# A decoder layer on one core: the feed-forward norm's root ahead of two projection copies, and three weight blocks' low parts subtracted on GpSimd

## The chip, the cores and the metric

The kernel runs on one core of a Trainium2 chip. The metric is the device time of one launch in microseconds, the median of several runs. The profile is one profiled execution; in its rows PE is TensorE (PEld its weight loads), DVE is VectorE, ACT is ScalarE, POOL is GpSimd and SP is SyncE, which only issues DMAs here.

## The reference

One decoder layer works on 512 prompt positions and 8 sample positions, 520 columns in all, with a width of 2048 and a feed-forward width of 5632. Cut to what matters here:

```python
def layer_out(h, o_sb, o_cm, p, g_out_sb, g_out_cm, w_out, g_ffn, w_gate, w_up, w_down,
              g_ple, w_ple_gate, w_ple_proj):
    o = jnp.concatenate([rmsnorm(o_sb, g_out_sb), rmsnorm(o_cm, g_out_cm)], axis=-1)
    h = h + o @ w_out
    f = rmsnorm(h, g_ffn)                # mean square over 2048 features, its root, then the gain
    h = h + (jax.nn.silu(f @ w_gate) * (f @ w_up)) @ w_down
    h = h + jax.nn.sigmoid(rmsnorm(h, g_ple) @ w_ple_gate) * (p @ w_ple_proj)
    return h
```

Before it, a mixer (attention and a gated MLP inside chunks) makes o_sb and o_cm. All is in fp32.

## The kernel before

**Layout.** Activations lie feature-major: 16 tiles of 128 features by 520 columns. Each fp32 number is split in a high part (fp32r, written by ScalarE) and a low part (the number less its high part, written by VectorE), for weights and activations alike; a product is then three matmuls: high by high, high by low, low by high. TensorE multiplies blocks of 128 by 128 by 260 columns.

**Order of the stages around the change.** After the output projection (TensorE L2113), `p @ w_ple_proj` is computed, 16 tiles of 12 matmuls (L2348, `plain_block`), while the residual's norm is finished. ScalarE copies each finished tile out of PSUM (`take_proj`, L1280) and GpSimd sends it to DRAM (L978). A tile n of TensorE waits for copy n-2. In the same time ScalarE squares the last residual tiles (`square_residual`, L1130) and multiplies them by the gain (`weigh_residual`, L1138); GpSimd has summed the first 15 squares in `h_sum`. TensorE sums over the partitions by matmuls with ones (L2459 for `h_sum`, L2460 for tile 15's squares), and ScalarE makes the root by Ln and Exp (L1420, L1421), which counts `root_done`.

**The first pair.** Gate and up tiles are computed in pairs, by a scheme of seven products (blocks 0 to 6 of a pair, `product`, L2364) in place of eight. Each product wants a weight block (128 by 1024) and an operand (half of the features by half of the columns), and both are sums or differences of halves. For the weights VectorE makes the sums (`add_weights`, L1825, into `w_sum` or the raw weights), ScalarE the high part (`high_pair`, L1293) and VectorE the low part (`low_pair`, through `low`, L1813). For the operands, once for the whole feed-forward part, VectorE scales f by the root (`scale_op`, L2004), combines quarters (`combine_op`, L2009), ScalarE makes the high part (`high_op`, L1285), VectorE the low part (`low_op`, L2016), all in two halves g = 0, 1. The order on VectorE and on ScalarE is written out by hand for the first pair. `pair_of_tiles` then runs for each pair; for the first one with `begun=True`, which leaves out what was written out by hand.

**Who waits for whom.** `lo_done` counts low parts of weights in order. TensorE waits for it before each product (`after_low`), VectorE before it writes over `w_sum` or a raw block, and SP before it loads the next weights into a raw slot. ScalarE writes block k's high part once product k-3 has ended, as three blocks fit into the buffer. TensorE's product 0, 1 and so on of a pair go into three accumulators, and product 2 waits until ScalarE has copied part 0 (`copy_part`, L1335). At the end of a gate tile ScalarE applies Silu (L1387 to L1390), with a load of its table, and then takes part 0 of the next pair.

Of the kernel before, what the change touches and what calls it, by code (L numbers as in the profile page):

```python
# [76 lines left out]
DOWN_COPIES = 5  # L77
PROJ_JOBS = 4
UNIT_JOBS = 7
DOWN_JOBS = 4 * UNIT_JOBS  # L80
CHUNK_COPIES = 4 * DOWN_COPIES

# [295 lines left out]
def build(nc, w_units, x_t, p_t, cache_k, cache_v, page_table, g_mix, g_out, g_ffn, g_ple, g_q, g_k,  # L378
# [6 lines left out]
    with ExitStack() as ctx:  # L385
# [156 lines left out]
        def raw(i):  # L542
            return raw_slot(LOADS[i].slot)
# [4 lines left out]
        def slot(w, job):  # L548

            first = JOB_POS[job] % SUBS * SUB  # L550
            return w[:, :, :].rearrange("p a n -> p (a n)")[:, first:first + JOB_SIZE[job] * SUB]
# [327 lines left out]
        def _(pool):  # L879
# [96 lines left out]
            for n in range(KT):  # L976
                pool.wait_ge(proj_taken, n + 1)
                pool.dma_start(proj_dram[:, n, :], proj_stage[:, n % STAGES, :]).then_inc(proj_out[n % STAGES], 16)  # L978
            def residual(u, row, half):

                first = 4 * u + 2 * row
                return h_dram[:, first:first + 2, half * HALF:(half + 1) * HALF]
# [37 lines left out]
        def _(act):  # L1020
# [106 lines left out]
            def square_residual(k):  # L1127

                act.wait_ge(h_final, k + 1)
                act.activation(f[:, k, :], h[:, k, :], ACT.Square).then_inc(sq_done, 1)  # L1130

            def weigh_residual(k):

                if k == KT - 1:
                    act.wait_ge(x_sum_ready, 4)
                else:
                    act.wait_ge(h_sum_done, k + 1)
                act.activation(f[:, k, :], h[:, k, :], ACT.Copy, scale=gain_ffn[:, k:k + 1]).then_inc(f_done, 1)  # L1138
# [136 lines left out]
            def take_proj(n):  # L1275

                act.wait_ge(ended, n + 1)
                if n >= STAGES:
                    act.wait_ge(proj_out[n % STAGES], 16 * (n // STAGES))
                act.activation(halves(proj_stage[:, n % STAGES, :]), tile_ps(n), ACT.Copy).then_inc(proj_taken, 1)  # L1280
# [130 lines left out]
            high_w(U_FFN + 1, 0)  # L1411
            weigh_residual(KT - 4)
            weigh_residual(KT - 3)
            take_proj(0)
            square_residual(KT - 1)
            weigh_residual(KT - 2)
            take_proj(1)
            take_proj(2)
            act.wait_ge(x_sum_ready, 4)
            chained(act.activation(halves(h_r[:, :]), pair, ACT.Ln, bias=eps[:, 0:1], scale=1.0 / D_MODEL))  # L1420
            act.activation(h_r[:, :], h_r[:, :], ACT.Exp, scale=-0.5).then_inc(root_done, 1)  # L1421
            take_proj(3)
            high(3, slot(w_hi, 3), raw_slot(3))
            take_proj(4)
# [75 lines left out]
        def _(dve):  # L1500
# [326 lines left out]
            def low_pair(item, k):  # L1827

                src = {0: raw(item.loads), 3: raw(item.loads + 3), 4: raw(item.loads + 1),
                       6: raw(item.loads + 2)}  # L1830
                low(item.jobs + k, src[k] if k in src else w_sum[:, :])
# [70 lines left out]
            def join(dst, x, w):  # L1902
                dve.tensor_tensor(dst, x, w, ALU.add).then_inc(joined, 1)

            def pair_of_tiles(item, after, acc, begun=False):
# [37 lines left out]
                dve.wait_ge(ended, item.end + 4)  # L1943
                dve.wait_ge(copied, 4 * item.n + 1)
                join(part[:, 0, :], part[:, 0, :], y_acc)
                begin(after, 1)
                dve.wait_ge(copied, 4 * item.n + 4)
                join(part[:, 2, :], part[:, 2, :], part[:, 3, :])
# [111 lines left out]
                combine_op(quad(1, 0, g), quad(0, 0, g), -1.0, quad(1, 0, g), 11 + g)  # L2060
            for g in range(2):
                low_op(4, g, quad(0, 1, g))
            low_pair(first, 4)
            for g in range(2):
                low_op(5, g, quad(1, 1, g))
            low_pair(first, 5)
            for g in range(2):
                low_op(6, g, quad(1, 0, g))
            low_pair(first, 6)

            for item, after in zip(ITEMS, ITEMS[1:]):
                if isinstance(item, Down):
# [33 lines left out]
        def _(pe):  # L2106
# [35 lines left out]
            def wait_free(free, reader):  # L2142
                if free[0]:
                    pe.wait_ge(*free[0])
                free[0] = reader
# [293 lines left out]
                    mm.then_inc(ended, 1)  # L2439


            pe.wait_ge(p_lo_done, 2)
            for n in range(KT):
                job = n // 4
                if n % 4 == 0:
                    after_low(job)
                if n < 2:
                    pe.wait_ge(out_read, T_FFN - 1 + n)
                else:
                    pe.wait_ge(proj_taken, n - 1)  # L2450
                for k in range(2):
                    plain_block(job, n % 4 * 2 + k, tile_ps(n), p_hi[:, k, :], p_lo[:, k, :], k == 0, k == 1)
                if n == 1:
                    pe.wait_ge(h_sum_done, KT - 1)
                    pe.wait_ge(sq_done, X_SQUARES + 3 * HEADS + KT)
                    wait_free(pair_free, (root_done, 4))
                    for a in range(2):
                        half = slice(a * HALF, (a + 1) * HALF)
                        pe.matmul(pair_ps[:, a, 0:HALF], ones[:, :], h_sum[:, half], start=True, stop=False)  # L2459
                        mm = pe.matmul(pair_ps[:, a, 0:HALF], ones[:, :], f[:, KT - 1, half], start=False, stop=True)  # L2460
                    mm.then_inc(x_sum_ready, 1)


            pe.wait_ge(root_done, 4)
# [131 lines left out]
```

## Time and profile before

| | us |
|---|---|
| median of 3 runs (2404.16 to 2405.17) | 2404.69 |
| the profiled execution's own time | 2404.58 |
| its span in the trace | 2402.8 |
| TensorE busy | 2369.7 |
| VectorE busy | 1777.4 |
| ScalarE busy | 1201.4 |
| GpSimd busy | 377.8 |

Times in the rows below are microseconds from the span's start. The own time is 1.78 us more than the span. The stretch of interest lasts from about 828 us, where the projection begins, to about 905 us, in the second pair.

### The profile page before, as it was taken

To read this page: it belongs to the slowest core of one execution; us is meant where nothing else is said; L and a number is where in the kernel's file an instruction comes from. 1 tells how busy PE (TensorE), PEld (TensorE's weight loads), DVE (VectorE), ACT (ScalarE), POOL (GpSimd) and SP (SyncE) were. 2 spreads that over 40 slices of the span, in tenths; PEclk is the share of its full clock that TensorE was granted. 3 is DMA by queue.
4 is the path that set the end of the run, shared out by engine and by line. 5 is a ranking of instruction groups with operands and counts; after the bars stand their busy time and mean duration, and the time that the engine had idled before them with its cause. 6 is when DMAs were issued, how large, how long until landed. Compare 5 with 4: busy or idle time off the path is not lost.

```text
span 2402.8 us, 46846 instructions
## 1 busy us (share of the span) xinstructions
PE 2369.7 (99%) x19392; PEld 2346.2 (98%) x19392; DVE 1777.4 (74%) x2209; ACT 1201.4 (50%) x1935; POOL 377.8 (16%) x364
## 2 busy tenths in 40 slices
PE   8999999999999989999999999999999999999999
PEld 7999999999999989999999999999999999999999
DVE  6379888876765498788888888888878787876333
ACT  6343445665643464545464546464646464545221
POOL 0001111111111300303030303030303030213000
PEclk9999999999999999999999999999999999999999
DMA  6255666554543533839383838484847474786323
GB/s 214 89 188 213 242 251 230 199 196 159 174 151 119 160 114 104 194 102 192 104 189 112 185 116 178 120 176 119 178 122 176 125 170 130 160 182 239 102 89 107
DMA packets 135589, 382.57 MB, mean 159 GB/s; under 512 B 14026, under 2 KB 58186, under 8 KB 126674
## 3 DMA queue, kind: packets, MB, share of 16 engines
q1 hardware_dynamic: 72450, 285.16, 35.0%
q0 software_dynamic: 62640, 94.28, 20.4%
q8 instruction: 154, 2.52, 0.4%
q14 instruction: 57, 0.47, 0.1%
q10 hardware_dynamic: 288, 0.14, 0.0%
HBM read 309.18 MB, written 73.55 MB: 159 GB/s over the span
## 4 chain that ended last, share of the span: by engine, by line
PE 84%; DVE 10%; ACT 2%; issue 2%; DMA 1%; SPq 0%; ACTq 0%; DVEq 0%
PE out_ps L2113 25%; PE tok_mix L2364 15%; PE pair_ps L2364 13%; PE out_ps L2348 10%; PE out_ps L2364 7%; PE out_ps L2437 4%; PE pair_ps L2437 2%; DVE w_sum L1825 2%; DVE w_lo L1813 2%; PE out_ps L2241 2%; PE pair_ps L2152 1%; ACT w_hi L1293 1%; DVE w_lo L1818 1%; PE tok_mix L2437 1%; DMA w_raw<-w_units 1%
## 5 line engine op out<-in xcount | busy, mean ns | idle before, releaser
L2113 PE MATMUL out_ps<-x_hi,w_hi 128*128 128x260 f32 x1792 | 376.4, 291 | 10.0 <-DVE w_lo L1662 7.8
L1293 ACT ACTIVATE w_hi<-w_sum 128x1024 fp32r<-128x1024 f32 (+1 forms) x252 | 215.4, 855 | 340.2 <-DVE w_sum L1825 243.9
L2113 PE MATMUL out_ps<-x_hi,w_lo 128*128 128x260 f32 x1792 | 361.8, 284 | 0.0
L2113 PE MATMUL out_ps<-x_lo,w_hi 128*128 128x260 f32 x1792 | 361.5, 283 | 0.0
L1813 DVE TENSOR_TENSOR w_lo<-w_sum,w_hi 128x1024 fp32r<-128x1024 f32 (+1 forms) x252 | 244.5, 970 | 136.1 <-ACT w_hi L1293 135.2
L1293 ACT ACTIVATE w_hi<-w_raw 128x1024 fp32r<-128x1024 f32 (+1 forms) x306 | 261.2, 865 | 135.1 <-PE out_ps L2348 102.7
L2364 PE MATMUL tok_mix<-op_hi,w_hi 128*128 128x260 f32 x1056 | 297.3, 281 | 2.1 <-ACT part L1335 1.9
L2364 PE MATMUL tok_mix<-op_hi,w_lo 128*128 128x260 f32 x1056 | 298.1, 282 | 0.0
L2364 PE MATMUL tok_mix<-op_lo,w_hi 128*128 128x260 f32 x1056 | 297.6, 282 | 0.0
L989 POOL DMA_DIRECT2D h_dram<-staging x110 | 146.7, 1460 | 927.5 <-DVE staging L1974 908.9
L2113 PEld LDWEIGHTS out_ps<-x_hi,w_hi 128*128 128x128 f32 x1792 | 279.2, 190 | 12.9 <-DVE w_lo L1662 7.8
L2113 PEld LDWEIGHTS out_ps<-x_hi,w_lo 128*128 128x128 f32 x1792 | 277.4, 189 | 0.0
L2113 PEld LDWEIGHTS out_ps<-x_lo,w_hi 128*128 128x128 f32 x1792 | 277.2, 189 | 0.0
L2364 PE MATMUL pair_ps<-op_hi,w_hi 128*128 128x260 f32 x880 | 249.1, 283 | 8.2 <-DVE op_lo L2016 5.0
L2364 PE MATMUL pair_ps<-op_hi,w_lo 128*128 128x260 f32 x880 | 249.5, 284 | 0.0
L2364 PE MATMUL pair_ps<-op_lo,w_hi 128*128 128x260 f32 x880 | 249.0, 283 | 0.0
L1813 DVE TENSOR_TENSOR w_lo<-w_raw,w_hi 128x1024 fp32r<-128x1024 f32 x172 | 209.3, 1221 | 44.9 <-ACT w_hi L1293 44.9
L2364 PEld LDWEIGHTS tok_mix<-op_hi,w_hi 128*128 128x128 f32 x1056 | 198.2, 188 | 2.6 <-ACT part L1335 2.1
L2364 PEld LDWEIGHTS tok_mix<-op_hi,w_lo 128*128 128x128 f32 x1056 | 198.4, 188 | 0.0
L2364 PEld LDWEIGHTS tok_mix<-op_lo,w_hi 128*128 128x128 f32 x1056 | 198.1, 188 | 0.0
L1033 ACT ACTIVATE w_hi<-w_raw 128x1024 fp32r<-128x1024 f32 x114 | 114.3, 1050 | 157.6 <-PE out_ps L2113 157.3
L2364 PEld LDWEIGHTS pair_ps<-op_hi,w_hi 128*128 128x128 f32 x880 | 166.3, 189 | 9.3 <-issue 7.4
(310 smaller groups left out, 6119.2 us busy)
## 6 DMA issues: line engine op xcount, KB each, us to landing
w_raw<-w_units SPq DMA_DIRECT2D x239, 512.0 KB, 4.2
w_raw<-w_units SPq DMA_DIRECT2D x57, 1024.0 KB, 5.0
w_fifth<-w_units SPq DMA_DIRECT2D x58, 512.0 KB, 4.1
h_dram<-staging POOLq DMA_DIRECT2D x110, 260.0 KB, 7.2
k_ring<-cache_k SPq DMA_DIRECT2D x50, 512.0 KB, 4.8
v_ring<-cache_v POOLq DMA_DIRECT2D x42, 512.0 KB, 4.7
h_dram<-part POOLq DMA_DIRECT2D x50, 260.0 KB, 7.1
q_dram<-staging POOLq DMA_DIRECT2D x40, 260.0 KB, 6.7
```

What stands on the lines that cost most here:

```text
L989: pool.dma_start(dst, stage(k), accum_op=op).then_inc(h_added[DOWN_SLOT[k]], 16)
L1033: act.activation(w_hi[:, u % 2, cols], w_raw[:, u % 2, cols], ACT.Copy).then_inc(hi_done, 1)
L1293: act.activation(dst, src, ACT.Copy).then_inc(hi_done, 1)
L1813: dve.tensor_tensor(slot(w_lo, job), src, slot(w_hi, job), ALU.subtract).then_inc(lo_done, 1)
L1818: dve.tensor_tensor(as_blocks(slot(w_lo, job)), src, as_blocks(slot(w_hi, job)), ALU.subtract)\
L1825: dve.tensor_tensor(dst, x, w, op).then_inc(w_summed, 1)
L2113: mm = pe.matmul(out_ps[:, 2 * (t % 2) + a, 0:HALF], w[:, u % 2, cols], x[:, a * HALF:(a + 1) * HALF], start=first and n == 0, stop=last a ...
L2152: mm = pe.matmul(pair_ps[:, a, 0:HALF], ones[:, :], x[:, a * HALF:(a + 1) * HALF], start=True, stop=True)
L2241: mm = pe.matmul(o_s_ps(u, b)[:, hd:hd + 1], v_slot(j)[:, hd * P:(hd + 1) * P], a_s[:, b % 3, at:at + 1], start=False, stop=j == pages[-1] ...
L2348: mm = pe.matmul(tile[:, a, :], w, x[:, a * HALF:(a + 1) * HALF], start=first and n == 0, stop=last and n == 2)
L2364: mm = pe.matmul(acc, w, x[:, g, :], start=fresh and g == 0 and n == 0, stop=g == GROUPS - 1 and n == 2, skip_group_check=True)
L2437: mm = pe.matmul(DOWN_BANKS[i][:, a, :], w, x, start=fresh and c == 0 and n == 0, stop=c == 1 and n == 2, skip_group_check=True)
```

## The change

1. ScalarE squares residual tile 15 before copy 0 instead of after it, and makes the root (Ln, Exp) before copies 1 and 2 instead of after them.
2. TensorE sums the squares after the first of the two blocks of projection tile 1 instead of after the second, and takes both halves of `h_sum` before it waits for tile 15's squares.
3. The low parts of the weight blocks 4, 5 and 6 of the first pair are subtracted by GpSimd, behind its 16 projection DMAs, instead of by VectorE. Each waits for the low part before it and for its own high part. VectorE no longer counts these three in `lo_done`, so it waits, in the first pair's `pair_of_tiles`, for block 6's before it makes the second pair's first one.

```diff
--- before.py
+++ after.py
@@ -77,6 +77,7 @@
 DOWN_COPIES = 5
 PROJ_JOBS = 4
 UNIT_JOBS = 7
+POOL_LOWS = 4
 DOWN_JOBS = 4 * UNIT_JOBS
 CHUNK_COPIES = 4 * DOWN_COPIES
 
@@ -976,6 +977,16 @@
             for n in range(KT):
                 pool.wait_ge(proj_taken, n + 1)
                 pool.dma_start(proj_dram[:, n, :], proj_stage[:, n % STAGES, :]).then_inc(proj_out[n % STAGES], 16)
+
+            first = ITEMS[0]
+            sources = {4: raw(first.loads + 1), 6: raw(first.loads + 2)}
+            for k in range(POOL_LOWS, UNIT_JOBS):
+                job = first.jobs + k
+                pool.wait_ge(lo_done, JOB0 + job)
+                pool.wait_ge(hi_done, JOB0 + job + 1)
+                pool.tensor_tensor(slot(w_lo, job), sources[k] if k in sources else w_sum[:, :], slot(w_hi, job),
+                                   ALU.subtract).then_inc(lo_done, 1)
+
             def residual(u, row, half):
 
                 first = 4 * u + 2 * row
@@ -1411,14 +1422,14 @@
             high_w(U_FFN + 1, 0)
             weigh_residual(KT - 4)
             weigh_residual(KT - 3)
+            square_residual(KT - 1)
             take_proj(0)
-            square_residual(KT - 1)
             weigh_residual(KT - 2)
-            take_proj(1)
-            take_proj(2)
             act.wait_ge(x_sum_ready, 4)
             chained(act.activation(halves(h_r[:, :]), pair, ACT.Ln, bias=eps[:, 0:1], scale=1.0 / D_MODEL))
             act.activation(h_r[:, :], h_r[:, :], ACT.Exp, scale=-0.5).then_inc(root_done, 1)
+            take_proj(1)
+            take_proj(2)
             take_proj(3)
             high(3, slot(w_hi, 3), raw_slot(3))
             take_proj(4)
@@ -1943,6 +1954,8 @@
                 dve.wait_ge(ended, item.end + 4)
                 dve.wait_ge(copied, 4 * item.n + 1)
                 join(part[:, 0, :], part[:, 0, :], y_acc)
+                if begun:
+                    after_low(item.jobs + UNIT_JOBS - 1)
                 begin(after, 1)
                 dve.wait_ge(copied, 4 * item.n + 4)
                 join(part[:, 2, :], part[:, 2, :], part[:, 3, :])
@@ -2060,13 +2073,10 @@
                 combine_op(quad(1, 0, g), quad(0, 0, g), -1.0, quad(1, 0, g), 11 + g)
             for g in range(2):
                 low_op(4, g, quad(0, 1, g))
-            low_pair(first, 4)
             for g in range(2):
                 low_op(5, g, quad(1, 1, g))
-            low_pair(first, 5)
             for g in range(2):
                 low_op(6, g, quad(1, 0, g))
-            low_pair(first, 6)
 
             for item, after in zip(ITEMS, ITEMS[1:]):
                 if isinstance(item, Down):
@@ -2439,6 +2449,19 @@
                     mm.then_inc(ended, 1)
 
 
+            def sum_residual():
+
+                pe.wait_ge(h_sum_done, KT - 1)
+                wait_free(pair_free, (root_done, 4))
+                for a in range(2):
+                    pe.matmul(pair_ps[:, a, 0:HALF], ones[:, :], h_sum[:, a * HALF:(a + 1) * HALF],
+                              start=True, stop=False)
+                pe.wait_ge(sq_done, X_SQUARES + 3 * HEADS + KT)
+                for a in range(2):
+                    mm = pe.matmul(pair_ps[:, a, 0:HALF], ones[:, :], f[:, KT - 1, a * HALF:(a + 1) * HALF],
+                                   start=False, stop=True)
+                mm.then_inc(x_sum_ready, 1)
+
             pe.wait_ge(p_lo_done, 2)
             for n in range(KT):
                 job = n // 4
@@ -2450,15 +2473,8 @@
                     pe.wait_ge(proj_taken, n - 1)
                 for k in range(2):
                     plain_block(job, n % 4 * 2 + k, tile_ps(n), p_hi[:, k, :], p_lo[:, k, :], k == 0, k == 1)
-                if n == 1:
-                    pe.wait_ge(h_sum_done, KT - 1)
-                    pe.wait_ge(sq_done, X_SQUARES + 3 * HEADS + KT)
-                    wait_free(pair_free, (root_done, 4))
-                    for a in range(2):
-                        half = slice(a * HALF, (a + 1) * HALF)
-                        pe.matmul(pair_ps[:, a, 0:HALF], ones[:, :], h_sum[:, half], start=True, stop=False)
-                        mm = pe.matmul(pair_ps[:, a, 0:HALF], ones[:, :], f[:, KT - 1, half], start=False, stop=True)
-                    mm.then_inc(x_sum_ready, 1)
+                    if n == 1 and k == 0:
+                        sum_residual()
 
 
             pe.wait_ge(root_done, 4)
```

## Rows read from the trace of the kernel before

**Rows 1.** The page, its span and part 1.

```profile
span 2402.8 us, 46846 instructions
...
PE 2369.7 (99%) x19392; PEld 2346.2 (98%) x19392; DVE 1777.4 (74%) x2209; ACT 1201.4 (50%) x1935; POOL 377.8 (16%) x364
```

**Rows 2.** Waits of TensorE, 830 to 897 us: in total, times, longest.

```profile
PE pair_ps L2364 <- DVE op_lo L2016: 5.0, 1, 5.0
PE tok_mix L2364 <- ACT part L1335: 1.9, 1, 1.9
```

**Rows 3.** Timeline of VectorE: start, us, instruction, count, idle before and its releaser.

```profile
837.17 4.70 DVE L2004 TENSOR_TENSOR f<-f,h_r 128x1040 f32<-128x1040 f32 x4 [2.79 <-ACT h_r L1421]
...
850.97 2.38 DVE L2016 TENSOR_TENSOR op_lo<-f,op_hi 128x1040 fp32r<-128x1040 f32 x2
...
866.01 1.22 DVE L1813 TENSOR_TENSOR w_lo<-w_fifth,w_hi 128x1024 fp32r<-128x1024 f32 x1
...
868.29 2.38 DVE L2016 TENSOR_TENSOR op_lo<-f,op_hi 128x1040 fp32r<-128x1040 f32 x2
...
875.20 1.22 DVE L1813 TENSOR_TENSOR w_lo<-w_raw,w_hi 128x1024 fp32r<-128x1024 f32 x1
...
883.21 1.22 DVE L1825 TENSOR_TENSOR w_sum<-w_raw,w_fifth 128x1024 f32<-128x1024 f32 x1
```

**Rows 4.** Timelines of ScalarE, then of TensorE.

```profile
831.07 0.63 ACT L1130 ACTIVATE f<-h 128x520 f32<-128x520 f32 x1
...
835.77 0.69 ACT L1420 ACTIVATE h_r<-pair_ps,eps 128x520 f32<-128x520 f32 x1
...
849.83 1.07 ACT L1285 ACTIVATE op_hi<-f 128x1040 fp32r<-128x1040 f32 x1
...
869.29 1.05 ACT L1293 ACTIVATE w_hi<-w_sum 128x1024 fp32r<-128x1024 f32 x1
875.30 1.06 ACT L1293 ACTIVATE w_hi<-w_raw 128x1024 fp32r<-128x1024 f32 x1 [4.96 <-PE pair_ps L2364]
...
890.06 1.06 ACT L1293 ACTIVATE w_hi<-w_sum 128x1024 fp32r<-128x1024 f32 x1 [4.49 <-DVE w_sum L1825]
...
831.81 0.67 PE L2459 MATMUL pair_ps<-h_sum,ones 128*128 128x260 f32 x2
...
833.44 0.59 PE L2348 MATMUL out_ps<-p_hi,w_hi 128*128 128x260 f32 x2
...
869.66 0.56 PE L2364 MATMUL pair_ps<-op_hi,w_hi 128*128 128x260 f32 x1 [4.96 <-DVE op_lo L2016]
...
894.13 0.39 PE L2364 MATMUL tok_mix<-op_hi,w_hi 128*128 128x260 f32 x1 [1.86 <-ACT part L1335]
```

**Rows 5.** Windows: us, busy time (instructions) of each engine, granted clock, DMA.

```profile
864.70:869.60 4.90, 0.00 (x1) 0.00 (x0) 4.90 (x6) 4.74 (x7) 0.00 (x0) 0.90 0.06 9
869.60:875.30 5.70, 5.54 (x24) 5.27 (x24) 5.70 (x6) 0.74 (x1) 0.00 (x0) 0.50 0.21 84
889.00:894.20 5.20, 3.33 (x29) 3.13 (x27) 2.21 (x2) 4.08 (x7) 0.00 (x0) 1.00 0.33 101
...
894.20:901.00 6.80, 6.80 (x57) 6.80 (x58) 4.72 (x4) 4.11 (x6) 0.00 (x0) 1.00 0.33 96
```

**Rows 6.** GpSimd: one line's durations (ns, min/median/max), and one row of the timeline.

```profile
L968 POOL TENSOR_TENSOR h_sum<-h_sum,h_sq x15: 1302/1307/2080, 2176.2 to 2214.5; 128x520 f32<-128x520 f32 x15
...
713.28 0.28 POOL L957 TENSOR_TENSOR y<-q 128x64 f32<-128x64 f32 x1 [18.93 <-DVE q L1581]
```

**Rows 7.** Timelines of GpSimd and VectorE where both work, at 460 and 820 us.

```profile
459.64 2.17 POOL L926 TENSOR_TENSOR sb_r<-sb_r,pool_sq 128x512 f32<-128x512 f32 x1
...
460.57 2.31 DVE L1513 TENSOR_TENSOR w_lo<-w_raw,w_hi 128x1024 fp32r<-128x1024 f32 x1
...
820.28 1.22 DVE L1513 TENSOR_TENSOR w_lo<-w_raw,w_hi 128x1024 fp32r<-128x1024 f32 x1
...
820.34 2.34 POOL L968 TENSOR_TENSOR h_sum<-h_sum,f 128x520 f32<-128x520 f32 x1 [7.82 <-ACT f L1130]
```

## Prediction

> **What bounds the kernel now.** I read the page's first part first: TensorE is busy for nearly the whole span [rows 1], so an edit pays only where it shortens a wait of TensorE. Its waits from 830 to 897 us come next. The two longest are 5.0 us behind the low parts of an operand (op_lo) and 1.9 us behind ScalarE's copy of a partial sum [rows 2]. Both lie in the stretch that the diff touches, the end of the projection and the first pair.
>
> The third view is VectorE's timeline. From 837.17 us, when it begins to scale f by the root, its instructions follow each other at a step of about 1.14 us (the next starts 0.08 before one of 1.22 ends); two scale, combine or low-part operations take 2.38 [rows 3]. It is without a pause until 890, where its third sum for the second pair ends. So the stretch is a chain of VectorE's. A product is 24 matmuls at 0.12 us (57 in 6.80 [rows 5]), 2.88 us of TensorE, and is done before VectorE has the next low part: product 3 starts at 869.66, when low_op(3, 0) of the row at 868.29 has ended [rows 3, 4]. At the end of the chain ScalarE's high part of the second pair's third block has waited 4.49 us for that third sum [rows 4]. Behind this high part stand, in ScalarE's queue, the Silu with its table load and the copy of part 0, and TensorE's third product of the second pair waits for that copy: it starts at 894.13 [rows 4]. The list of waits has nothing longer behind it in this stretch. **What the change does to this start at 894.13 is what it does to the time.**
>
> The clock is the fourth view. TensorE idles from 864.70, the granted clock falls to 0.50, the 1.2 GHz level, and product 3 takes 5.54 us at it [rows 5]. That is hidden: product 4 waits for VectorE anyway.
>
> **Part 1: the root two copies earlier.** Before, the Ln starts at 835.77, right behind take_proj(2), and Ln and Exp take 1.4 us together, up to VectorE's start at 837.17 [rows 3, 4]. After: the square of tile 15, before at 831.07 behind take_proj(0), runs first, from about 830.6 to 831.2. TensorE begins the sum after 6 of tile 1's 12 matmuls, 0.72 us (6 by 0.12) ahead of the 831.81 of before; the four matmuls of the sum take 1.63, up to 833.44 [rows 4]. So they are done near 832.8, with ScalarE hearing of it at about 833.0, and the root comes at 834.4. VectorE had been idle for 2.79 us before 837.17 [rows 3], so it is free from 834.38 and starts some 2.7 us earlier.
>
> What is late next is ScalarE, whose copies are paced by TensorE's projection tiles (1.44 us each), and these do not move: high_op(1, 1) is the second L1285 in that stretch, 849.83 to 850.90, behind copy 11 and a high part [rows 4]. VectorE's low part of it was second in the pair that begins at 850.97, due at 852.11 [rows 3]; it can now start at 850.93, no earlier. So **1.2 us of the 2.7 arrive** (bounds: 0.6, if ScalarE came later by one copy of 0.6; 2.7, if its queue moved along). The copies that now stand behind the root end at about 834.9 and 835.5; TensorE needs the first for tile 3, at 834.9, and the second for tile 4, at 836.3: at most 0.1 us. I take 0, since those tiles are done long before VectorE's chain asks for product 0. If the cover were gone, 0.1 is what it would cost.
>
> **Part 2: three subtractions leave VectorE.** Blocks 4, 5 and 6, the first at 875.20, cost a step of 1.14 each on its chain [rows 3]: 3 x 1.14 = **3.4 us less**.
>
> **Part 3: the same three on GpSimd.** The trace has none of that shape and output. The nearest: 520 elements with nothing beside them take 1.307 us, 64 elements 0.28 [rows 6]; (1.307 - 0.28) / 456 = 2.25 ns an element, so 1024 take about 2.44 us. The output is fp32r there and f32 in the rows; as bounds I keep 1.31 (the 520-element row itself) and 4.9 (twice the 2.44).
>
> What this does to VectorE decides, and the trace has it. At 459.64 GpSimd starts 512 elements while VectorE subtracts, and takes 2.17 us, not 1.3. VectorE's next subtraction, of the very shape in question, takes 2.31 us instead of 1.22 [rows 7]: 1.09 longer, nearly the whole of GpSimd's operation. At 820.34 the other side is seen: VectorE's 1.22 is untouched, GpSimd needs 2.34, since it came second and no further instruction of VectorE's was due [rows 7]. They take turns: GpSimd waits for VectorE's instruction, then VectorE's next one waits for GpSimd's. In the stretch at hand VectorE always has a next one, and its scale, combine, low and weight operations all read two tensors of SBUF. A block then holds it for 1.09 + 512 x 0.00225 = 2.24 us, **3 x 2.24 = 6.7 us more** where 3.4 were taken out.
>
> The Trainium skill says this outright (SBUF — State Buffer, section "SBUF: two separate sides"): the port pair that the two share is locked for a whole instruction, against a vector operation with two SBUF inputs too. By that rule the sum is the one below; without it, that of the first rival. Its GPSIMD Engine Reference, section "Elementwise — side-by-side cycle accounting", gives 4497 ns for 2048 fp32 elements, as an estimate 2.25 us for 1024; holds 0.2 shorter would make the sum +1.5.
>
> **The walk.** Low part 3 ended at 867.23 [rows 3], now near 866.0, and releases block 4. VectorE is in the next sum by then, until 867.1; GpSimd holds from there to 869.3, and low_op(3, 0) ends at 870.5: product 3 starts 0.9 later than before. Block 5 needs ScalarE's high part, 869.29 to 870.34 before [rows 4], now done near 869.4, and has its turn right behind; low_op(3, 1) ends at 873.8. Block 6 needs high part 6, which waits for product 3 (875.30 before [rows 4], now 876.5): GpSimd from 878.4 to 880.6. VectorE's first sum for the second pair, 883.21 to 884.43 before [rows 3], now ends near 886.4 in place of 884.4. The wait added ahead of the second pair's first low part is for block 6, by then 6 us old: free. Were it late, VectorE's joins, sums and low parts of the second pair would all stand behind it, and TensorE behind them. SP's loads that wait for blocks 4 and 6 go out earlier, and nothing waits for them. GpSimd's own queue is empty: the copies' DMAs are out before product 1, the accumulating ones come several products later. From 886.4 on the chain is the same work as before, and 894.13 becomes about 896.2.
>
> **Sum:** -1.2 (root) - 3.4 (off VectorE) + 6.7 (held) = **+2.1 us**. The profiled execution took 2404.58 us, 1.78 more than its span and 0.11 below the median of the runs, 2404.69; +2.1 on this median is 2406.8. A difference within 0.2% (4.8 us) is about what a measurement of this kernel cannot tell from no change.
>
> **Rivals.**
> - *No hold.* GpSimd's work lies beside VectorE's and the path gets all of parts 1 and 2: -1.2 - 3.4 = -4.6, so 2400.1, faster. For it: the step at 820.28 that stayed 1.22. Against it: the 2.31 [rows 7]. It decides for faster once a block holds VectorE for under 1.5 us ((3.4 + 1.2) / 3). Chance 0.08.
> - *Two holds of three.* One block finds VectorE in a pause: +2.1 - 2.2 = -0.1, so 2404.6, and up to 2405.4 where only a part of one is saved. For it: GpSimd's start depends on ScalarE and TensorE. Against it: VectorE's timeline has no pause there. Chance 0.12.
> - *The clock falls once more.* TensorE's wait before product 3 grows to about 7 us, hidden as before; that before the late copy from 1.9 to about 2.5. A wait of 1.9 left the clock at 1.00, one of 5.0 brought 0.50 [rows 5]. Should 2.5 be enough, one or two products behind it at 5.54 in place of 2.88 cost 2.7 to 5.3 with nothing to hide them: 2409.4 to 2412.0. Chance 0.10.
> - *GpSimd is slower with this output.* At twice 2.44 three blocks add 7.3: 2414.0; a quarter more gives +1.8, 2408.5. Chance 0.06.
>
> **Chances and range.** The forecast has the other 0.64, with a range of its own of 2405.4 to 2408.2 (holds of 2.0 to 2.6, root of 0.6 to 1.4). The range of 8 in 10 adds the two-holds case and the near half of the clock case and leaves out the rest: 2402.8 to 2410.0. Faster by over 0.2% needs the first rival and a little more: 0.04. Slower by over 0.2% is the far half of the clock case and most of the slow output: 0.10. Within: 0.86.
>
> **What would show it.** The Ln at 833.0 and VectorE's first scaling at 834.4; the low part of operand 1's second half at 850.9; three GpSimd subtractions of 2.4 us, longer by what they wait first; three VectorE rows of about 3.4 us in place of 1.22; a wait of about 7 us before product 3; the second pair's third product at 896. VectorE rows that all stay at 1.2 would prove me wrong towards faster; a second stretch at clock 0.50 near 896, or GpSimd rows of 4 us with nothing beside them, towards slower.

## The result, and the profile after

The changed kernel takes 2408.49 us in the median of 22 runs (2407.94 to 2411.74), the kernel before 2405.68 in 22 runs beside them (2404.13 to 2407.52). The ratio is 1.0015, 95% interval 1.0009 to 1.002: 2 to 5 us slower, 3.6 by the ratio's middle. That is within the 0.2% for which the prediction said "within", though the interval reaches up to that line. The median lies in the range of 8 in 10 (2402.8 to 2410.0) and 1.7 us over the forecast of 2406.8; 1.0 of these 1.7 is that the kernel before, too, took longer in these runs than the 2404.69 that the forecast started from. The profiled execution has this page:

```profile
span 2406.2 us, 46850 instructions
...
PE 2370.2 (99%) x19392; PEld 2347.0 (98%) x19392; DVE 1776.9 (74%) x2206; ACT 1201.1 (50%) x1935; POOL 400.2 (17%) x367
```

TensorE's waits over the whole span, longest first (total, times, longest). The row of 1.9 us behind ScalarE's copy [rows 2] has shrunk to 0.2, the 5.0 us behind op_lo are the same, and in front of both stands a wait that the kernel before did not have, for a low part on GpSimd:

```profile
PE pair_ps L2374 <- POOL w_lo L987: 7.9, 1, 7.9
...
PE pair_ps L2374 <- DVE op_lo L2029: 5.0, 1, 5.0
...
PE tok_mix L2374 <- ACT part L1346: 0.2, 1, 0.2
```

VectorE's timeline. It starts to scale f at 834.32 in place of 837.17 [rows 3]; the second low part of operand 1 begins at 850.81 after a pause; and from 866.98 to 878.59 it runs ten instructions at their usual 1.24 us, none of them longer. One detail will matter: the row at 854.27 ends at 855.49, so VectorE stands still for 0.04 us before 855.53, and not again until 878.59. At 866 it is in its tenth instruction since then.

```profile
834.32 4.69 DVE L2017 TENSOR_TENSOR f<-f,h_r 128x1040 f32<-128x1040 f32 x4
...
850.81 1.24 DVE L2029 TENSOR_TENSOR op_lo<-f,op_hi 128x1040 fp32r<-128x1040 f32 x1 [1.16 <-ACT op_hi L1296]
...
854.27 1.22 DVE L1824 TENSOR_TENSOR w_lo<-w_sum,w_hi 128x1024 fp32r<-128x1024 f32 x1
855.53 1.22 DVE L1836 TENSOR_TENSOR w_sum<-w_sum,w_raw 128x1024 f32<-128x1024 f32 x1
...
866.98 2.39 DVE L2029 TENSOR_TENSOR op_lo<-f,op_hi 128x1040 fp32r<-128x1040 f32 x2
869.29 2.39 DVE L2022 SCALAR_TENSOR_TENSOR f<-f 128x1040 f32<-128x1040 f32 x2
871.59 7.00 DVE L2029 TENSOR_TENSOR op_lo<-f,op_hi 128x1040 fp32r<-128x1040 f32 x6
883.35 3.40 DVE L1836 TENSOR_TENSOR w_sum<-w_raw,w_fifth 128x1024 f32<-128x1024 f32 x1 [4.77 <-POOL w_lo L987]
```

GpSimd's three subtractions, in the same columns. The first one is asked for at 866.02, when low part 3 is there, and ends at 880.78. That is 2.2 us after VectorE's last instruction of the stretch, and it did not get a single turn before. The other two, with VectorE at rest when they start, take 2.36 and 2.37 us. Only VectorE's weight sum at 883.35 is held, behind the third (3.40 in place of 1.22):

```profile
866.02 14.76 POOL L987 TENSOR_TENSOR w_lo<-w_raw,w_hi 128x1024 fp32r<-128x1024 f32 x1 [10.08 <-DVE w_lo L1824]
880.86 2.36 POOL L987 TENSOR_TENSOR w_lo<-w_sum,w_hi 128x1024 fp32r<-128x1024 f32 x1
883.30 2.37 POOL L987 TENSOR_TENSOR w_lo<-w_raw,w_hi 128x1024 fp32r<-128x1024 f32 x1
```

ScalarE's root starts at 832.92 in place of 835.77, and the high part for which VectorE pauses is where it was [rows 4]:

```profile
832.92 0.69 ACT L1429 ACTIVATE h_r<-pair_ps,eps 128x520 f32<-128x520 f32 x1 [0.70 <-PE pair_ps L2461]
...
849.72 1.06 ACT L1296 ACTIVATE op_hi<-f 128x1040 fp32r<-128x1040 f32 x1
```

The chain that ended last, in order of time (start, length, what), for the stretch around the change. Before, VectorE worked up to the second pair with no pause above 0.04 us, and this view follows it, except from 869.66 to 880.05, where it names the products 3 and 4 beside it. Now it leaves VectorE at 866, goes through GpSimd's first subtraction, and then through TensorE's products 4 and 5, for the end of which the next high part waits:

```profile
866.02 14.78 POOL w_lo L987
...
880.88 5.08 PE pair_ps L2374 x24
885.96 2.90 PE tok_mix L2374 x24
...
888.96 1.07 ACT w_hi L1304
...
893.63 1.01 ACT w_hi L1304
...
894.71 1.28 ACT L1398
...
897.26 0.40 ACT part L1346
...
897.70 0.39 PE tok_mix L2374
```

The windows show what product 4 costs on that chain (columns as in [rows 5]). TensorE stands still for 7.8 us, and of the 24 matmuls behind it most run at the lower clock:

```profile
868.30:873.00 4.70, 4.58 (x24) 4.39 (x24) 4.70 (x5) 0.74 (x1) 4.70 (x1) 0.65 0.28 106
873.00:880.80 7.80, 0.00 (x0) 0.00 (x0) 5.59 (x5) 3.00 (x3) 7.78 (x1) 0.63 0.00 0
880.80:885.80 5.00, 4.92 (x25) 4.95 (x25) 2.45 (x1) 0.00 (x0) 4.73 (x2) 0.55 0.34 105
885.80:888.70 2.90, 2.90 (x27) 2.90 (x26) 2.56 (x4) 1.33 (x2) 0.00 (x0) 1.00 0.53 174
```

To compare executions whose projection begins at different times (828.41 to 830.34 in the fourteen kernels), I use one length: from the projection's first matmul to the start of the second pair's third product, both in TensorE's timeline. It is 894.13 - 828.94 = 65.19 us before and 897.70 - 828.81 = 68.89 after, **3.70 us more**. What follows until the end of the span is 1508.7 us before and 1508.5 after, so all of the difference lies in this length.

### The profile page after: what moved, and what is told of

The parts are those of the page before. It is cut to its first block, busy times and chain, and to the rows that moved or that the text cites. A ratio compares the mean times of both kernels' runs of the same rounds, so it can differ in the third digit from the quotient of the medians.

```text
span 2406.2 us, 46850 instructions
## 1 busy us (share of the span) xinstructions
PE 2370.2 (99%) x19392; PEld 2347.0 (98%) x19392; DVE 1776.9 (74%) x2206; ACT 1201.1 (50%) x1935; POOL 400.2 (17%) x367
## 4 chain that ended last, share of the span: by engine, by line
PE 84%; DVE 9%; ACT 3%; issue 2%; DMA 1%; POOL 1%; SPq 0%; ACTq 0%; DVEq 0%
PE out_ps L2123 25%; PE tok_mix L2374 16%; PE pair_ps L2374 13%; PE out_ps L2358 10%; PE out_ps L2374 8%; PE out_ps L2447 3%; PE pair_ps L2447 2%; DVE w_sum L1836 2%; DVE w_lo L1824 2%; PE out_ps L2251 2%; ACT w_hi L1304 1%; DVE w_lo L1829 1%; PE pair_ps L2162 1%; PE tok_mix L2447 1%; DVE staging L1987 1%
```

## The experiments

All lengths in one table. "Length" is the one just defined, "rest" what follows it, both from one profiled execution. The ratio is to runs of the kernel before beside each kernel, whose medians lie between 2405.27 and 2405.68, with its 95% interval; where there is none, the kernel ran once.

| kernel | median us | ratio | length | against before | rest |
|---|---|---|---|---|---|
| before | 2405.68 | | 65.19 | | 1508.7 |
| changed | 2408.49 | 1.0015 (1.0009 to 1.002) | 68.89 | +3.70 | 1508.5 |
| root alone | 2404.28 | 0.9996 (0.9987 to 1.0005) | 64.02 | -1.17 | 1508.5 |
| GpSimd alone | 2409.10 | 1.0019 (1.001 to 1.0028) | 69.53 | +4.34 | 1508.6 |
| VectorE waits for its own low_op(3, 0) | 2407.48 | 1.0009 (0.9999 to 1.0018) | 67.12 | +1.93 | 1508.7 |
| low_op(3, 1) ready late | 2409.52 | 1.0015 (1.0006 to 1.0024) | 69.41 | +4.22 | 1508.7 |
| high parts ahead | 2403.85 | 0.9995 (0.9986 to 1.0004) | 62.47 | -2.72 | 1508.7 |
| GpSimd just at work | 2408.15 | one run | 69.13 | +3.94 | 1508.6 |
| asked for later | 2409.17 | one run | 69.38 | +4.19 | 1508.6 |
| in quarters | 2408.62 | one run | 69.59 | +4.40 | 1508.6 |
| standstill at 866.8 | 2408.71 | one run | 67.29 | +2.10 | 1510.0 |
| standstill at 860.8 | 2408.34 | one run | 67.25 | +2.06 | 1509.9 |
| two blocks on GpSimd | 2406.82 | 1.0006 (0.9997 to 1.0016) | 66.73 | +1.54 | 1508.2 |
| high parts and Silu ahead | 2400.73 | 0.9982 (0.9973 to 0.9991) | 60.84 | -4.35 | 1508.5 |

### The two parts by themselves

The root alone is the changed kernel with the three subtractions back on VectorE:

```diff
             for g in range(2):
                 low_op(4, g, quad(0, 1, g))
+            low_pair(first, 4)
             for g in range(2):
                 low_op(5, g, quad(1, 1, g))
+            low_pair(first, 5)
...
+            low_pair(first, 6)
...
-                if begun:
-                    after_low(item.jobs + UNIT_JOBS - 1)
```

> Parts 2 and 3 undone: the three subtractions are VectorE's again, the earlier root stays. All theories agree on the place: VectorE's first scaling at 834.3, the low part of operand 1's second half at 850.8, everything behind it 1.1 to 1.2 us earlier than before, the second pair's third product at 893.0. Time 1.2 us under the kernel before (0.9 to 1.5). If the root alone were worth its whole 2.8 us, it would be 2.8 under.

Measured: 1.17 us less in length. VectorE's and TensorE's rows of this kernel: VectorE waits for ScalarE's high part, as in the changed kernel, and the third product of the second pair starts at 892.94.

```profile
850.92 1.24 DVE L2018 TENSOR_TENSOR op_lo<-f,op_hi 128x1040 fp32r<-128x1040 f32 x1 [0.81 <-ACT op_hi L1287]
...
892.94 0.39 PE L2366 MATMUL tok_mix<-op_hi,w_hi 128*128 128x260 f32 x1 [1.62 <-ACT part L1337]
```

GpSimd alone is the kernel before with the subtractions moved and the root left where it was, that is parts 1 and 2 of the diff taken back.

> The root stays where it was before, only the three subtractions move to GpSimd. Theory A (GpSimd gets no turn as long as VectorE's next instruction is ready when GpSimd asks): its first subtraction is asked for near 867.2, ends near 882, and is one row of about 15 us; time 4.5 to 5 us over the kernel before. Theory B (they take turns, as forecast): three rows of VectorE of 3.4 us, 3.3 over the kernel before.

Measured: 4.34 us more in length, a little under the 4.5 to 5 of theory A. The first row is 14.77 us long, again up to the end of VectorE's chain, so the turns of the forecast do not happen. The two parts add up: -1.17 + 4.34 = 3.17, against 3.70 for both. The other 0.5 is product 4, which takes 4.4 us here (clock 0.63) and 4.9 in the changed kernel (0.55).

```profile
866.97 14.77 POOL L986 TENSOR_TENSOR w_lo<-w_raw,w_hi 128x1024 fp32r<-128x1024 f32 x1 [11.19 <-DVE w_lo L1823]
```

### When does GpSimd get its turn?

In [rows 7] it had got one between two VectorE subtractions with no pause between them, here it got none between ten. VectorE's row of [rows 7] in full shows the two subtractions, and that VectorE had stood still for 0.36 us right before them:

```profile
458.95 3.94 DVE L1513 TENSOR_TENSOR w_lo<-w_raw,w_hi 128x1024 fp32r<-128x1024 f32 x2 [0.36 <-ACT w_hi L1033]
```

Seven kernels ask what differs. First, one wait more on VectorE:

```diff
-            for g in range(2):
-                low_op(3, g, quad(1, 0, g))
+            low_op(3, 0, quad(1, 0, 0))
+            dve.wait_ge(op_lo_done, 7)
+            low_op(3, 1, quad(1, 0, 1))
```

> The changed kernel, with one wait more on VectorE: low part 3's second half waits for the first half to be finished. Theory A (turn only where VectorE's next instruction was not ready when GpSimd asked) and theory C (turn only where VectorE stands still for a moment) both expect GpSimd's first subtraction to get in at about 868.3 and to end at 870.5 (a row of 4.5 us in place of 14.8), VectorE's second half to take 3.4 us, and the second subtraction, asked for at 870.6, to be the one that waits until VectorE's chain ends near 880.8. Product 4 then starts near 875, product 5 near 883; time 0.5 to 1 us under the changed kernel. Theory D (an operation of this size or output never gets a turn in a busy VectorE): first row still about 14.8 us, time as the changed kernel.

Theory D falls: an operation of this size and output does get in. The wait makes VectorE stand still for 0.04 us at 868.55; GpSimd takes its turn there, and low_op(3, 1) takes 3.29 us. What I did not expect is that the other two subtractions then got their turns too, inside the running chain, at once (rows of 3.25 and 3.30 us), and the length is 1.8 us under the changed kernel's, not 0.5 to 1:

```profile
866.35 4.43 POOL L987 TENSOR_TENSOR w_lo<-w_raw,w_hi 128x1024 fp32r<-128x1024 f32 x1 [10.08 <-DVE w_lo L1824]
870.86 3.25 POOL L987 TENSOR_TENSOR w_lo<-w_sum,w_hi 128x1024 fp32r<-128x1024 f32 x1
875.26 3.30 POOL L987 TENSOR_TENSOR w_lo<-w_raw,w_hi 128x1024 fp32r<-128x1024 f32 x1 [1.15 <-ACT w_hi L1304]
...
868.59 3.29 DVE L2029 TENSOR_TENSOR op_lo<-f,op_hi 128x1040 fp32r<-128x1040 f32 x1
```

Next, low_op(3, 1) waits for ScalarE instead, for something that comes after GpSimd has asked and before VectorE's running instruction ends:

```diff
-            for g in range(2):
-                low_op(3, g, quad(1, 0, g))
+            low_op(3, 0, quad(1, 0, 0))
+            dve.wait_ge(op_hi_done, 12)
+            low_op(3, 1, quad(1, 0, 1))
```

> The changed kernel, but low part 3's second half waits for ScalarE's last high part of operand 5, which ends near 867.8: after GpSimd has asked (866.0) and before VectorE's running instruction ends (868.2), so that VectorE never stands still. Theory A: GpSimd gets its turn at 868.2, its first row is about 4.5 us, VectorE's second half takes 3.4 us. Theory C (VectorE must stand still): no turn, first row still 14.8 us, VectorE's rows all 1.24. Theory D: as C.

The high part ends at 869.36, after the 867.56 at which GpSimd asks and 0.4 us before low_op(3, 0) ends. Still VectorE goes on without a pause, at its usual 1.24 us, and GpSimd's row is 14.77 us. So theory A falls as it was set out for this run: a wait at the same place as in the run before, but without a standstill, changes nothing. In its strict words (no turn as long as VectorE's next instruction is ready when GpSimd asks) this kernel does not test it, since at 867.56 low_op(3, 0) was next and ready; the kernels with a standstill ahead of the request, below, do.

```profile
867.56 14.77 POOL L987 TENSOR_TENSOR w_lo<-w_raw,w_hi 128x1024 fp32r<-128x1024 f32 x1 [10.07 <-DVE w_lo L1824]
...
868.31 1.05 ACT L1296 ACTIVATE op_hi<-f 128x1040 fp32r<-128x1040 f32 x1
...
869.68 1.24 DVE L2029 TENSOR_TENSOR op_lo<-f,op_hi 128x1040 fp32r<-128x1040 f32 x1
```

Three more change GpSimd's side; the listing has all three, shortened. "Just at work" writes 64 zeros first; "asked for later" waits for one more high part; "in quarters" cuts each subtraction in four:

```diff
                 pool.wait_ge(hi_done, JOB0 + job + 1)
+                if k == POOL_LOWS:
+                    pool.memset(h_sum[:, 0:64], 0.0)          # just at work
...
+                if k == POOL_LOWS:
+                    pool.wait_ge(op_hi_done, 11)              # asked for later
...
+                for i in range(4):                            # in quarters
+                    cols = slice(i * 256, (i + 1) * 256)
+                    ins = pool.tensor_tensor(slot(w_lo, job)[:, cols], src[:, cols], slot(w_hi, job)[:, cols],
+                                             ALU.subtract)
```

> The changed kernel, and GpSimd writes 64 zeros (into a scratch row that is free by then) directly ahead of its first subtraction. The turns that GpSimd got between two VectorE instructions were all asked for within about 1 us of GpSimd's own last work; the one of 14.8 us came after 10 us of rest. Theory W (a GpSimd that has just worked gets its turn): the first subtraction ends near 869 to 871 in place of 880.8, and VectorE shows a row of 3.3 us. Theory C (only after VectorE has stood still for a moment): first row still 14 to 15 us.

> The changed kernel, but GpSimd's first subtraction also waits for ScalarE's high part of operand 5's first half, about 866.8: it is asked for 0.8 us later within VectorE's instruction, still after 10 us of rest. If only the moment within VectorE's instruction mattered, it gets its turn at 868.2. By theories W and C alike it does not, and ends at 880.8, with a row of about 14 us.

> The changed kernel, with each subtraction on GpSimd in four instructions of 256 columns. By theory C the first quarter waits like the whole did, until VectorE's chain ends (878.6), and the rest follow: block 4 done at 881. By theory W the first quarter waits as long, the others have no VectorE to fight with. If short operations were let in where long ones are not, the quarters end near 868 to 873 and VectorE has several rows of about 1.8 us.

GpSimd's rows of the three kernels. A memset right ahead changes nothing, so theory W falls:

```profile
865.94 0.15 POOL L988 MEMSET h_sum<- 128x64 f32 x1 [10.04 <-DVE w_lo L1826]
866.05 14.68 POOL L989 TENSOR_TENSOR w_lo<-w_raw,w_hi 128x1024 fp32r<-128x1024 f32 x1
```

The later request came at 867.73, 0.05 us after the start of VectorE's next instruction and not, as I had meant, late in one. So it tests another moment than planned, and the answer for this one is again no turn (the changed kernel asked 0.17 us after the start of one):

```profile
867.73 13.75 POOL L989 TENSOR_TENSOR w_lo<-w_raw,w_hi 128x1024 fp32r<-128x1024 f32 x1 [11.09 <-ACT op_hi L1298]
```

The first quarter waits just as long, until 879.1, so an operation of a quarter of the size gets no turn either:

```profile
865.97 13.15 POOL L990 TENSOR_TENSOR w_lo<-w_raw,w_hi 128x256 fp32r<-128x256 f32 x1 [10.06 <-DVE w_lo L1828]
```

Left was VectorE's own past. In every turn seen so far it was within a few instructions of a standstill or of having been held. "Standstill at 866.8" puts one right before GpSimd asks, "standstill at 860.8" one five instructions earlier, and there is none after the request in either:

```diff
             begin(first, 3)
+            after_low(first.jobs + 2)                         # standstill at 860.8
...
             low_pair(first, 3)
+            after_low(first.jobs + 3)                         # standstill at 866.8
             last_sum(first)
```

> The changed kernel, but VectorE waits for its own low part 3 to be finished before it adds the next weight sum. It stands still for some 0.04 us at 865.9, just before GpSimd asks, and not again. Theory Y (what counts is how long VectorE has run without standing still or being held: in all the turns seen without a pause, it was in its first or second instruction since one): GpSimd gets its turn at 867.0, with a first row of about 3.3 us and a VectorE row of 3.3. Theory C (VectorE must stand still after GpSimd has asked): the first row is 14.8 us as in the changed kernel.

Measured, VectorE's rows and then GpSimd's: VectorE resumes at 866.86, GpSimd asks at 866.91, and at 868.00 it is VectorE that is held, for 3.39 us. The same happens to the next one, and at 879 once more. Theory C falls (nothing stood still after the request), and so does theory A in its strict words (low_op(3, 0), whose high part had long been there, was ready when GpSimd asked); theory Y stands:

```profile
866.86 1.23 DVE L1836 TENSOR_TENSOR w_sum<-w_sum,w_fifth 128x1024 f32<-128x1024 f32 x1
...
868.00 3.39 DVE L2029 TENSOR_TENSOR op_lo<-f,op_hi 128x1040 fp32r<-128x1040 f32 x1
...
866.91 3.38 POOL L987 TENSOR_TENSOR w_lo<-w_raw,w_hi 128x1024 fp32r<-128x1024 f32 x1 [10.08 <-DVE w_lo L1824]
870.37 3.25 POOL L987 TENSOR_TENSOR w_lo<-w_sum,w_hi 128x1024 fp32r<-128x1024 f32 x1
878.72 2.88 POOL L987 TENSOR_TENSOR w_lo<-w_raw,w_hi 128x1024 fp32r<-128x1024 f32 x1 [5.10 <-ACT w_hi L1304]
```

This is the kernel that behaves as the prediction's walk has it: turn for turn, and its length is 2.10 us over before, which is the prediction's sum. And it shows the third rival at work, behind the length measured: TensorE waits 2.1 us for the late copy (1.9 before), the clock is at 1.00 until then, and over the product that follows its mean is 0.62, so 4.4 us of TensorE in place of 2.88. Of these 1.5 us, 1.3 are left at the end, in "rest":

```profile
889.00:896.90 7.90, 5.89 (x48) 5.68 (x48) 5.06 (x6) 3.92 (x7) 0.00 (x0) 1.00 0.21 68
896.90:901.40 4.50, 4.42 (x24) 4.42 (x25) 3.49 (x3) 2.20 (x4) 0.00 (x0) 0.62 0.02 5
```

> The changed kernel, with VectorE's one standstill (waiting for its own low part 2) moved further ahead, to 860.1: when GpSimd asks at 866.0, VectorE is in its sixth instruction since. With the standstill one instruction before, GpSimd got its turn; with one ten instructions before it did not; a fourth instruction was still interrupted. If a count or a time of uninterrupted running decides, this run halves the open interval: the first row is 3.4 us if six instructions (5.9 us) are still few enough, 14.8 us if not. If a standstill makes VectorE open to GpSimd only for the few next instructions because of what they are, the row is 14.8 us too.

The standstill is 0.03 us ahead of the scaling at 860.82, and GpSimd, in the sixth VectorE instruction since, gets its turn with a row of 3.26 us. It asked 0.17 us after the start of VectorE's instruction, as in the changed kernel, so the moment within the instruction is not the difference. The open interval is now from the sixth to the tenth instruction, or 5.9 to 10.5 us of uninterrupted running. A hold counts like a standstill: the third subtraction, asked for at 878.54, came in VectorE's twelfth instruction (17.7 us) since the standstill but in the fourth since a hold, and got its turn too:

```profile
860.82 2.40 DVE L2017 TENSOR_TENSOR f<-f,h_r 128x1040 f32<-128x1040 f32 x2
...
866.74 3.26 POOL L987 TENSOR_TENSOR w_lo<-w_raw,w_hi 128x1024 fp32r<-128x1024 f32 x1 [10.17 <-DVE w_lo L1824]
```

### Fewer blocks

`POOL_LOWS = 5` in place of 4, with `low_pair(first, 4)` back on VectorE behind operand 4's low parts.

> The changed kernel with block 4 given back to VectorE; GpSimd subtracts only blocks 5 and 6. It asks for block 5 near 875.1, when four low parts of operands are still to come without a pause. By theories Y and C it waits for their end at 879.5, block 5 is done at 881.8 (a row of 6.5 to 7 us) and block 6 at 884.2; the wait of 7.9 us before product 4 is gone, the second pair's third product starts near 895, 1 us over before. If it was something about block 4 that kept it waiting, block 5's row is under 4 us.

It was not something about block 4: block 5, asked for in the middle of the chain at 876.66, waits for its last four instructions, the first of them at work, and its row is 6.72 us. The length was 1.54 over before, a little more than expected; product 4 started 2.2 us late behind VectorE's own low part (2.3 with the root alone), and product 5 2.1 us late behind GpSimd's.

```profile
876.66 6.72 POOL L987 TENSOR_TENSOR w_lo<-w_sum,w_hi 128x1024 fp32r<-128x1024 f32 x1 [19.25 <-DVE w_lo L1824]
```

### Two other orders on ScalarE

The first takes up the 1.5 us that the earlier root lost behind ScalarE. It is the root alone with another order on ScalarE:

```diff
             take_proj(9)
-            take_proj(10)
             high_op(1, 0, quad(0, 0, 0), 4)
+            take_proj(10)
+            high_op(1, 1, quad(0, 0, 1), 4)
             take_proj(11)
             high_pair(first, 1)
-            high_op(1, 1, quad(0, 0, 1), 4)
-            for n in range(12, KT):
-                take_proj(n)
-            for g in range(2):
-                high_op(2, g, quad(0, 0, g), 8)
+            take_proj(12)
+            take_proj(13)
+            high_op(2, 0, quad(0, 0, 0), 8)
+            take_proj(14)
+            high_op(2, 1, quad(0, 0, 1), 8)
+            take_proj(15)
```

> The kernel with the earlier root alone, and ScalarE's high parts of operands 1 and 2 moved ahead of projection copies 10 and 11, 14 and 15. If it was ScalarE's queue that ate 1.5 of the root's 2.8 us, VectorE's pause of 1.2 us before the low part at 850.8 is gone, its chain runs 2.6 to 2.8 us earlier than before at every row behind it, and the time is 2.4 to 2.8 us under the kernel before. If something else is next (a copy that comes late for TensorE's tiles), it is 1.2 under as with the root alone.

ScalarE's row and VectorE's: the pause is gone (both low parts in 2.38 us), and the length is 2.72 less. The medians show 1.5 us less, with an interval on the ratio that takes in none and 3.4 alike.

```profile
846.94 1.06 ACT L1287 ACTIVATE op_hi<-f 128x1040 fp32r<-128x1040 f32 x1
...
847.72 2.38 DVE L2020 TENSOR_TENSOR op_lo<-f,op_hi 128x1040 fp32r<-128x1040 f32 x2
```

The second adds a look at the chain's end. ScalarE waits 4.49 us for a weight sum [rows 4] and only then loads the table and applies Silu, although Silu's inputs are there before:

```diff
                 after_end(item.end + 7)
-                highs(item.end + 7)
+                if not begun:
+                    highs(item.end + 7)
...
                     act.activation(yg[:, 1, HALF:TOK], part[:, 2, :], ACT.Silu, scale=-1.0).then_inc(silu_done, 1)
+                if begun:
+                    highs(item.end + 7)
```

> The kernel of the run with ScalarE's high parts ahead (no subtraction on GpSimd), and in the first pair ScalarE applies Silu, with its table load, before the second pair's third high part, for which it waits 4.5 us anyway. The copy of part 0 then follows the high part at 887.9 in place of 890.4; the second pair's third product starts at 889.1, held by its low part, in place of 890.9: 1.8 us less, 4.4 to 4.6 us under the kernel before. If Silu's inputs come too late for that, as much less.

ScalarE's rows, then TensorE's: the table is loaded at 882.68 inside the wait, and the third product starts at 889.56, held by its low part for the last 0.2 us. The length is 4.35 less than before, and the median 2400.73, ratio 0.9982 (0.9973 to 0.9991): 2.2 to 6.5 us faster than the kernel before, and its median is 7.8 us under the changed kernel's.

```profile
882.68 1.28 ACT L1390 ACT_TABLE_LOAD   x1
...
887.10 1.06 ACT L1295 ACTIVATE w_hi<-w_sum 128x1024 fp32r<-128x1024 f32 x1 [1.90 <-DVE w_sum L1832]
...
889.56 0.36 PE L2371 MATMUL tok_mix<-op_hi,w_hi 128*128 128x260 f32 x1 [0.22 <-DVE w_lo L1820]
```

## Why the prediction was right, and where it was not

**What bounds, and where it ends up.** Right. The whole difference lies before the second pair's third product, and the rest is 1508.5 to 1508.7 us in both. TensorE's waits ahead of it differ by 0.3 us at most.

**Part 1, the root.** Right in each step: VectorE starts 2.85 us earlier (2.72 counted from the projection's first matmul), ScalarE's high part at 849.72 stops it, and 1.17 us arrive, for a forecast of 1.2. The kernel with the high parts ahead shows that it was ScalarE's order that ate the rest.

**Part 2, the subtractions taken off VectorE.** The size was right: VectorE's chain of operands ends at 878.59, 3.4 us earlier than before counted from the projection's first matmul, which is the root's 1.17 and the two subtractions of 1.14 that stood ahead of its end. That it would shorten the path was not, since the path went to the blocks themselves.

**Part 3, GpSimd's price.** 2.44 us from the two rows, 2.36 measured, so the fp32r output cost nothing more, and the fourth rival falls. A whole hold of VectorE was forecast at 2.24 and is 3.40 - 1.22 = 2.18.

**The step that failed is "they take turns".** From [rows 7] I took it for the general case. In this chain GpSimd gets none: VectorE passes from one instruction to the next ten times over, for 12.6 us from the request on, and GpSimd's operation is served when VectorE rests. So the sentence on block 4 ("GpSimd holds from there to 869.3") was wrong by 11.5 us, and with it the walk behind it: product 3 starts 1.3 us earlier than before, not 0.9 later, and product 4 waits 7.9 us, for GpSimd. The sum came out near by another way. In place of three holds inside VectorE's chain (6.7 us) there are two subtractions after it, up to 883.2, and a third beside a held weight sum up to 886.75; and TensorE's products 4 and 5 are now on the path, product 4 with 4.9 us at a clock of 0.55 in place of 2.88. The path's weight sum ends at 886.75 in place of 884.43 [rows 3], 2.3 us later, and by then it is not even the last: the high part of the second pair's second block waits for the end of product 5, and its low part starts at 890.05, where VectorE's timeline of before has it at 886.49. So of these 3.6 us some 1.3 come from product 4's clock (an estimate: 3.6 less the 2.3 of the weight sum, which would have been last with product 4 at 2.88). The 3.6 us are handed on unchanged to 897.70. That the time lies in the stated range all the same is luck: the length's +3.70 is made of other terms than the forecast's +2.1. With turns, in the kernel with a standstill at 866.8, the length is +2.10, the prediction's own sum. The prediction also says that VectorE has no pause until 890, and passes over the 0.04 us at 855.5 (856.8 in the kernel before) from which the ten instructions count.

**The bounds.** By the prediction's own terms, holds of 2.0 to 2.6 and a root of 0.6 to 1.4, its narrower range would be 2405.9 to 2408.5; it has 2405.4 to 2408.2.

**The rivals.** "No hold" was half the truth: VectorE was not held in the chain, but the path did not get the gain. It had no place for a GpSimd that is kept waiting, so it would have forecast the sign wrong. "Two holds of three" had only VectorE's side: two of the blocks did find VectorE at rest and only one held it, but nothing was saved, since TensorE waited for the blocks themselves. "The clock falls once more" came true in another place than I named: the longer wait, now before product 4, is on the path, and there the lower level costs. In the place that I named it needs the turns, and there a wait of 2.1 us had it behind it.

**The Trainium skill's rule.** The Trainium skill (SBUF — State Buffer, section "SBUF: two separate sides") states a lock on the shared port pair for a whole instruction, held by whichever of the two starts first. VectorE's 3.40 at 883.35 agrees, as GpSimd had started 0.05 us before. The rule is about one instruction against another and does not say who is next when VectorE has more of them queued, so it neither forecasts nor contradicts GpSimd's 14.76. Turns between the two were my own reading of [rows 7], not the Trainium skill's.

**What stays open.** A standstill of VectorE, of 0.03 us, up to five instructions before GpSimd asks gave GpSimd turns, and so did having been held; ten instructions of running did not. Whether a count, a time or something else in the chip draws the line between six and ten, and why, no run shows. The rows of each kernel are of one profiled execution, and both kernels with a standstill ahead of the request ran once. The kernel "asked for later" was to test another moment within the instruction and missed it.

## What to carry to other kernels

A subtraction of two SBUF tensors on GpSimd does not lie beside a VectorE that is busy with operations on two SBUF tensors of its own: it either holds VectorE for its own 2.2 us, where VectorE would have needed 1.14, or it waits until VectorE rests, here 12 us. Give it such work only where VectorE's timeline has a pause as long as the operation, and look who waits for the result. When a stall is removed, look in the same profile for the next queue that is late, and for waits (the 4.49 us of ScalarE here) into which work queued behind them fits: reordering ScalarE brought more than moving work did.

## What was not expected of the hardware

- VectorE and GpSimd do not always take turns: one operation of GpSimd waited 12.4 us through ten VectorE instructions that each started 0.08 us before the last one's end, and this in four kernels with a row of 14.7 to 14.8 us, 13.75 where it asked later in the chain, 13.15 for a quarter of the size.
- One standstill of 0.03 us on VectorE, even 5.9 us before the request, was followed by turns one for one: VectorE's held rows took 3.4 us, GpSimd's 3.2 to 3.4, and 2.7 to 2.9 for the third block, which asked later within a VectorE instruction.
- Waits of TensorE of 2.1 to 2.3 us, with others ahead of them, had the 1.2 GHz level at their end or behind it in four kernels: before product 4 with the root alone (2.3, then 4.4 us at a clock of 0.65), before products 4 and 5 with two blocks, near 895 in the two kernels with a standstill. Waits of 1.9 us, before and with the high parts ahead, had not.
